# Two reorderings inside the layer norms of a float32 transformer kernel: the additions of squares behind the low halves, and one weight conversion ahead of two half tiles

## The reference, cut to what matters

```python
def layernorm(x, g, b):
    xf = x.astype(jnp.float32)
    mu = jnp.mean(xf, axis=-1, keepdims=True)
    var = jnp.mean(jnp.square(xf - mu), axis=-1, keepdims=True)
    y = (xf - mu) * lax.rsqrt(var + LN_EPS)
    return (y * g + b).astype(x.dtype)
...
    x = layernorm(DEEPNORM_ALPHA * x + mix, ln1_g, ln1_b)
    hid = jnp.square(jax.nn.relu(jnp.einsum('bsd,df->bsf', x, w_ff1)))
    ff = jnp.einsum('bsf,fd->bsd', hid, w_ff2)
    return layernorm(DEEPNORM_ALPHA * x + ff, ln2_g, ln2_b)
```

## Time and profile before

| | |
|---|---|
| median of 3 runs | 2085.1 us (2084.9 to 2085.11) |
| the profiled execution: its own time, its span | 2085.24 us, 2083.3 us |
| PE busy with matmuls | 2051.0 us, 98% of the span |
| DVE, ACT, POOL busy | 1098.9 us (53%), 923.0 us (44%), 150.8 us (7%) |
| granted TensorE clock, mean | 0.998 of full speed |
| DMA | 101 GB/s on average |

### The profile page before, as it was taken

The page is one execution under the profiler, slowest core; times in us unless marked ns, Lnnn a source line. Parts: engine busy times, 40 slices in busy tenths (PEclk is TensorE's granted clock), DMA queues, the critical chain, the costliest instruction groups (busy, mean ns, idle before and its releaser), DMA issues. The chain is left out here.

```text
span 2083.3 us, 24654 instructions
## 1 busy us (share of the span) xinstructions
PE 2051.0 (98%) x9744; PEld 1691.8 (81%) x9744; DVE 1098.9 (53%) x1794; ACT 923.0 (44%) x1502; POOL 150.8 (7%) x207
## 2 busy tenths in 40 slices
PE   9999999999999999999999999999999999999997
PEld 6888788888888888788688888888888788888886
DVE  6655566565343444477586333337677586333336
ACT  5664334334232322366357243343566347233243
POOL 0000000000000000354000000000353000000000
PEclk9999999999999999999999999999999999999999
DMA  7332222333323322632332333322632332332321
GB/s 241 98 105 62 81 66 96 123 100 122 104 98 101 101 81 62 182 113 85 117 102 84 99 101 101 101 85 58 179 102 79 117 101 85 108 99 93 101 81 41
DMA packets 201518, 211.37 MB, mean 101 GB/s; under 512 B 7803, under 2 KB 181115, under 8 KB 201404
## 3 DMA queue, kind: packets, MB, share of 16 engines
q1 hardware_dynamic: 194544, 194.13, 29.9%
q0 software_dynamic: 6352, 15.24, 2.8%
q10 hardware_dynamic: 508, 0.43, 0.1%
HBM read 194.55 MB, written 8.95 MB: 98 GB/s over the span
## 5 line engine op out<-in xcount | busy, mean ns | idle before, releaser
L303 PE MATMUL ps<-Phi,wh 128*128 128x512 f32 (+1 forms) x1200 | 475.9, 397 | 9.3 <-DVE Plo L1291 5.0
L306 PE MATMUL ps<-Phi,wl 128*128 128x512 f32 (+1 forms) x1200 | 455.2, 379 | 0.6 <-DVE wl L272 0.6
L305 PE MATMUL ps<-Plo,wh 128*128 128x512 f32 (+1 forms) x1200 | 454.5, 379 | 0.0
L272 DVE TENSOR_TENSOR wl<-stage,wh 128x1024 fp32r<-128x1024 f32 x249 | 303.6, 1224 | 71.0 <-ACT wh L269 55.7
L269 ACT ACTIVATE wh<-stage 128x1024 fp32r<-128x1024 f32 (+2 forms) x252 | 260.2, 1041 | 172.1 <-PE ps L306 157.8
L303 PEld LDWEIGHTS ps<-Phi,wh 128*128 128x128 f32 x1200 | 226.2, 189 | 58.2 <-issue 19.2
L306 PEld LDWEIGHTS ps<-Phi,wl 128*128 128x128 f32 x1200 | 225.6, 188 | 44.5 <-DVE wl L272 1.0
L305 PEld LDWEIGHTS ps<-Plo,wh 128*128 128x128 f32 x1200 | 226.3, 189 | 40.6 <-issue 4.1
L303 PE MATMUL ps<-Qhi,wh 128*128 128x512 f32 (+1 forms) x680 | 256.5, 377 | 0.8 <-DVE Qlo L459 0.8
L306 PE MATMUL ps<-Qhi,wl 128*128 128x512 f32 (+1 forms) x680 | 254.4, 374 | 0.0
L305 PE MATMUL ps<-Qlo,wh 128*128 128x512 f32 (+1 forms) x680 | 254.4, 374 | 0.0
(11 more groups left out here) (303 smaller groups left out, 2935.4 us busy)
## 6 DMA issues: line engine op xcount, KB each, us to landing
stage<-in_w_ff SPq DMA_DIRECT2D x64, 1024.0 KB, 5.3
stage<-in_w_in SPq DMA_DIRECT2D x39, 1024.0 KB, 5.2
stage<-in_w_up SPq DMA_DIRECT2D x16, 1024.0 KB, 5.3
stage<-in_w_down SPq DMA_DIRECT2D x16, 1024.0 KB, 5.1
stage<-in_w_in SPq DMA_DIRECT2D x30, 512.0 KB, 4.8
stage<-in_w_out SPq DMA_DIRECT2D x12, 1024.0 KB, 5.1
stage<-in_w_bg SPq DMA_DIRECT2D x4, 1024.0 KB, 5.2
vrev<-H SPq DMA_DIRECT2D x2, 2048.0 KB, 13.0
```

What stands on the lines that cost most here:

```text
L272: t_lo = V.op(lambda e: e.tensor_tensor(lo, src, hi.bitcast(F32), ALU.subtract), st_landed[n, part], t_hi, w_free[u], sem=s_wlo)
L303: PE.op(lambda e: e.matmul(o, hi[:, k, c], x.hi[:, kx, tok], start=first, stop=False), t_hi, t_x or x.t[kx], list(waits), signal=False)
L305: PE.op(lambda e: e.matmul(o, hi[:, k, c], x.lo[:, kx, tok], start=False, stop=False), signal=False)
L306: return PE.op(lambda e: e.matmul(o, lo[:, k, c], x.hi[:, kx, tok], start=False, stop=last), t_lo, sem=s_wpe, signal=last)
```

## The change

It has two parts. In `last_three`, for the three norms with `nxt`, the additions of squares of half B (tiles 5, 6 and 7) are no longer made inside `part`, but later: those of tiles 5 and 6 behind `lows(0)`, `minus(5)`, `times(2)` and `lows(1)` of half A, that of tile 7 behind `times(3)` and `lows(2)`. And up to three `prepare()` stand ahead of `part(0, 0)`, where before up to that many pieces were converted behind `part(1, 0)`.

```diff
-            def deviate(self, k, sl):
+            def deviate(self, k, sl, add=True):
...
                 self.pending.append((k, sl, s, t))
-                if len(self.pending) > 1:
+                if add and len(self.pending) > 1:
                     self.add()
...
-                norm.late(j, sl, then)
-
+                norm.late(j, sl, then, add)
+
+            for _ in range(3 if nxt else 0):
+                if state["prep"] < state["use"] + 3:
+                    prepare()
             part(0, 0, range(8))
             part(1, 0, range(8))
             while nxt and state["prep"] < state["use"] + 3:
...
             A_.times(0)
             A_.minus(4)
             A_.times(1)
-            part(1, 1, range(8))
+            part(1, 1, range(8), add=False)
             A_.lows(0)
             A_.minus(5)
             A_.times(2)
             A_.lows(1)
+            norm.add()
             A_.minus(6)
-            part(2, 1, range(8))
+            part(2, 1, range(8), add=False)
+            A_.times(3)
+            A_.lows(2)
             norm.add()
             B_.sums()
-            A_.times(3)
-            A_.lows(2)
```

More of the change, by code:

```diff
@@ L1224, in add, with late @@
                     sq_free[k % 2] = self.acc2
-            def late(self, j, sl, summed=True):
+            def late(self, j, sl, summed=True, add=True):
                 if summed:
@@ L1230, in late @@
                                     t_h[j], self.acc)
-                self.deviate(j, sl)
+                self.deviate(j, sl, add)
         class Half:
@@ L1301, in last_three, with part @@
             A_, B_ = (Half(norm, sl, vg, vb, nxt is not None) for sl in halves)
-            def part(p, hf, ks, then=True):
+            def part(p, hf, ks, then=True, add=True):
                 sl, (i, w), b = halves[hf], tail[p], (low, high)[hf][p]
```

## The result

| | before | after |
|---|---|---|
| median | 2085.0 us (20 runs, 2084.28 to 2087.68) | 2082.11 us (20 runs, 2081.74 to 2083.6) |
| the profiled execution: own time, span | 2085.24 us, 2083.3 us | 2083.13 us, 2081.1 us |

The ratio is 0.9986, with a 95% interval of 0.998 to 0.9993: 2.9 us less. The interval leaves out 1, so this is a difference; it is smaller than the 0.2% that the prediction took for no change. The forecast was 2082.3 us.

What follows compares the result with a forecast made beforehand. PE is busy 2051.0 of 2083.3 us, but the DVE and ACT chain paces half A. Three norms at 0.78 us (2.34) plus 0.48 for the conversion give 2.82 us: 2082.3 us forecast, range 2081.0 to 2084.2.

Steps and rivals of the forecast that it cites:

- What bounds: Half A of each norm: PE waits for lows(0), but the whole chain of DVE and ACT sets the pace.
- The additions, 0.78 us a norm: Three norms: with the additions postponed, qB and half B start 0.78 us sooner; 2.34 us in all.
- Why not 0.99: lows(0) wins 0.99 us; waits of 0.23, 0.49 and about 0.2 go, two additions on end cost 0.11 more; 0.78 remains.
- the walk: The prediction's step-by-step laying out of the new instruction order on DVE and ACT, with start times from the profile's rows.
- PE's new waits: Half A of each norm: about 0.2 us before tile 0, 0.4 before tile 2, a new 0.3 before tile 4.
- The conversion, 0.48 us: Norm 3: converting earlier starts H of tile 7 and the mean's matmul 0.48 us sooner; wait for accq about 0.9.
- The sum, 2.82 us: Whole kernel: 2.34 us from the additions plus 0.48 from the conversion.
- The rule weighed: DVE: the page has dependent additions cost nothing extra, 0.33 us more gain, 2082.0 us; the prediction followed the trace's 0.11 us.
- Gain given back later: Rival, chance 0.12: PE meets an independent wait at half B or the feed-forward product; 2084.4 to 2085.1 us.
- PE's waits go altogether: Rival, chance 0.05: DVE overlaps more than 0.34 us a step; up to 6.4 us gained, 2078.7 us.
- The additions hold up a square: Rival, chance 0.01: postponed additions free the sq buffers too late for tile 7's square; time back towards 2085.1 us.
- Slower through the conversion: Rival, chance 0.02: in norm 3 a late load or slot delays wh, wl and the mean's matmul; 2089.3 us.

Runs made afterwards that it cites:

- e5b: Against the kernel before: of the change only the additions of tiles 5 and 6 moved; 0.12 us gained per norm, 2084.95 us (1 run).
- e6b: Against the kernel before: of the change only the addition of tile 7 moved; 0.57 us gained per norm, 2084.51 us (1 run).
- e4b: Against the changed kernel: ACT writes half B's muB ahead of H and Phi of half A's tile 4; 2079.25 us, ratio 0.9971 to the kernel before.
- e2b: Against the kernel before: only the conversion moved, additions left in place; wait for accq 0.91 us for 1.38, 2085.5 us (1 run).
- e8b: Against e4b: minus(6) between the additions of tiles 5 and 6, half B's times(0) ahead of its minus(5, 6, 7); 2078.87 us.
- e7b: Against the changed kernel: norm 3's conversion one half tile later, between tiles 5 and 6; wait for accq 2.29 us, 2084.14 us (1 run).
- e1b: Against the kernel before: only the additions moved, conversion left in place; 0.69 us gained per norm, 2083.06 us, ratio 0.999.
- e3b: The changed kernel run again, unaltered, beside others on one chip; 2082.2 us, ratio 0.9985 to the kernel before.

## Why the prediction was right

The time of 2082.11 us lies 0.2 us under the forecast of 2082.3, in its range of 2081.0 to 2084.2 and in the forecast's own of 2081.7 to 2083.1. That it is as close as 0.2 us is in part luck: by the intervals the gain is 0.25 us smaller than forecast, by the medians 0.1 us larger. Point by point:

- *What bounds*: that PE waits for `lows(0)` but the chain of DVE and ACT paces half A held. e5b and e6b show it: removing the longest wait alone moves it to tile 2, and removing a shorter one further on gives most of the gain.
- *The additions, 0.78 us a norm*: 0.70 measured. The order of every row came as walked, and the one mis-sized term is the distance of two additions of which the second needs the first: I took 0.45 us from a pair of other instructions; the two hold DVE 0.87 us with the next one 0.34 after, so 0.53. That is the 0.08. All three norms agree.
- *Why not 0.99*: here the number came out right but the reason given for it did not. The prediction adds the printed idles, 0.23 and 0.49 us. From start to start the three waits of the kernel before cost 0.31, 0.57 and 0.18 us over the 0.34 of an independent step, and the walk's own `lows(3)` is 0.97 us sooner (1094.95 for 1095.92), 0.90 in the trace. What takes it down to 0.7 is ACT: `muB` stands behind `H` and `Phi` of tile 4 there, so `qB` waits 1.05 us instead of 0.86, and 0.19 us of DVE's gain are lost at that place. This is the wait that e4b removes.
- *PE's new waits*: 0.2, 0.4 and 0.3 us forecast before tiles 0, 2 and 4; 0.19 and 0.40 in the trace, and at tile 4 no idle is printed, but it starts 0.55 us behind the two of `L1266` (1096.32 to 1096.87) where it took 0.25 (1098.23 to 1098.48 before), 0.30 us more.
- *The conversion, 0.48 us*: 0.47 (1.38 to 0.91), and e2b has it alone.
- *The sum, 2.82 us*: 2.57 by the intervals, 2.9 and 3.0 by the medians of two sets of runs. The medians' last 0.3 to 0.4 us are within what they vary by; I can't assign them.
- *The rule weighed*: the page "VectorE: DVE Perf Modes" of the Trainium skill, section "The DRAIN you can't avoid", reports of eight copies in a row that a semaphore after each cost nothing extra; the same section says that an instruction that is not held back starts earlier. The trace agrees with the second: independent instructions of 0.42 us start 0.34 apart. It does not agree with the first: between two dependent additions it is 0.53 us, 0.19 more, and e8b takes it out: 0.19 us a norm. The measurement decides, against the page, at this size.
- *Gain given back later*: not seen in the medians, which differ by no less than the intervals gained. Profiled executions do lose at the start of the third layer, but e2b, with nothing to give back, waits 2.4 us for the DMA there. That the wait changes between executions of one program is shown (2.15 and 0.58 us); what makes the DMA late, and why the clock falls behind some of these waits and not behind others, was not tried.
- *PE's waits go altogether*: no, 1.8 us for `Plo` and 0.9 for `accq` remain. *The additions hold up a square*: no, the square of tile 7 waits for its `d` on DVE alone (1.61 us of idle before 1092.59).
- *Slower through the conversion*: not by a late load; `wh` starts as soon as the squares are through. e7b shows that one place further down the code the same conversion costs norm 3 more than it gains.

## What to carry to other kernels

When an engine waits on a chain of two others, don't price a reordering by the first wait that it shortens. Lay the new order down row by row, with the waits as they will be, up to the point where the waiting engine has room again, and take the difference there; here 0.99 us at the first wait were 0.70 at the end, and a move that left the first wait alone was worth 0.57. Then look for the next thing to move among the idles on the chain's own engines, not on the engine that waits for it: the 1.05 us of DVE before `qB` were worth 0.94 us a norm, more than the 0.70 of the additions.

## What the runs showed of the hardware

- Two additions of 256 float32 columns in a row on DVE, the second on the first's result, start 0.53 us apart (0.95 us for the pair less 0.42 for one); independent instructions 0.34. A `H`, `accq` pair, dependent too, starts 0.45 apart. One independent instruction between the additions hides all of it.
- ACT passes from `muB`, a copy out of PSUM of 0.37 us, to the next instruction in 0.39 us.
- The first score matmul of the third layer waits 0.58 us for its DMA in one execution of the changed kernel and 2.15 us in another. The nine traces other than that of the kernel before all have this wait, from 0.58 to 2.52 us.
- Behind that wait the granted TensorE clock fell to half (1.2 GHz) in five of the nine traces (the change's first, e2b, e6b, e7b, e8b; waits of 2.15, 2.39, 2.52, 1.71 and 1.45 us) and not in the other four (e1b, e3b, e4b, e5b; 1.29, 0.58, 1.37 and 2.20 us). The eight matmuls behind it take 3.48 us instead of 1.92. So a single profile's time can move by 1 us and more without an edit; the interval within the stretch that was edited agreed within 0.01 us between the two traces of the change (22.20 and 22.21).
